# Two edits at a fused transformer kernel's layer hand-overs: order of the low parts, and the last unit by halves

## The reference

```python
# first block
x = x + merged @ w_out                                          # end of hand-over q = 0's input
x = x + square(relu(rmsnorm(x, norm2_g) @ w_up)) @ w_down       # q = 1
# second block, for layer l = 0, 1
x = x + 0.5 * rms_norm(swiglu(rms_norm(x, ng[0]), w_gu, w_down), ng[1])   # q = 2, 5
h = rms_norm(x, ng[2])
mix = concatenate([tok, mem_out]) @ w_o
x = x + rms_norm(mix, ng[3])                                    # q = 3, 6
x = x + 0.5 * rms_norm(swiglu(rms_norm(x, ng[4]), w_gu, w_down), ng[5])   # q = 4, 7
```

## Time and profile before

| | |
|---|---|
| executions | 1473.56, 1477.7, 1473.89 us |
| median | 1473.89 us |
| span of the profiled execution (first to last instruction) | 1470.6 us |
| time of the profiled execution itself | not told by the profile; only its span is |
| mean granted PE clock over the span | 0.982 of full speed |
| PE busy | 1401.7 us, 11538 matmuls |
| DVE, ACT, POOL busy | 922.4, 732.0, 192.7 us |

### The profile page before, as it was taken

One profiled execution on the slowest core, in us unless ns is written; L12 is line 12 of the kernel. 1 busy time (PEld: TensorE's weight loads), 2 busy tenths in 40 slices (PEclk: granted clock), 3 DMA queues, 4 the chain that ended last, 5 costly groups with the idle time before them and its releaser, 6 DMA issues.

```text
span 1470.6 us, 28247 instructions
## 1 busy us (share of the span) xinstructions
PE 1401.7 (95%) x11538; PEld 1358.3 (92%) x11538; DVE 922.4 (63%) x1368; ACT 732.0 (50%) x1205; POOL 192.7 (13%) x210
## 2 busy tenths in 40 slices
PE   5899899999999999999998999999999989899998
PEld 5878799999999999998898999999999987899998
DVE  7998786666535665556765665556564467565644
ACT  7712755544435454455446454455444364554443
POOL 0465000022000111013101111011110010111100
PEclk9899899999999999999999999999999989999999
DMA  9223324455554555544342555544555341345551
GB/s 372 105 103 116 127 86 174 159 204 185 194 185 160 177 195 191 195 173 155 135 144 99 190 197 189 198 172 172 188 198 199 146 170 58 109 178 195 192 200 58
DMA packets 36815, 244.33 MB, mean 166 GB/s; under 512 B 4208, under 2 KB 5360, under 8 KB 8816
## 3 DMA queue, kind: packets, MB, share of 16 engines
q1 hardware_dynamic: 34992, 238.17, 44.7%
q10 hardware_dynamic: 1728, 4.81, 0.9%
HBM read 241.67 MB, written 1.05 MB: 165 GB/s over the span
## 4 chain that ended last, share of the span: by engine, by line
PE 81%; DVE 9%; ACT 5%; issue 2%; POOL 2%; DMA 1%; SPq 0%; DVEq 0%; ACTq 0%; POOLq 0%
PE ps L1891 49%; PE ps L1931 26%; DVE wlo L1083 3%; PE ps L2114 1%; PE ps L2140 1%; ACT whi L592 1%; DVE alo L1478 1%; PE ps L2130 1%; DMA xtok<-in_xt 1%; POOL pr L1809 1%; POOL pr L1808 1%; PE ps L2019 1%; ACT junk L829 1%; DVE yr L1456 0%; ACT pP L782 0%
## 5 line engine op out<-in xcount | busy, mean ns | idle before, releaser
L1083 DVE TENSOR_TENSOR wlo<-raw,whi 128x1024 fp32r<-128x1024 f32 (+1 forms) x434 | 505.1, 1205 | 273.3 <-ACT whi L592 273.2
L1891 PE MATMUL ps<-ahi,whi 128*128 128x256 f32 x2112 | 599.5, 284 | 32.1 <-DVE wlo L1083 18.0
L592 ACT ACTIVATE whi<-raw 128x1024 fp32r<-128x1024 f32 (+1 forms) x434 | 427.2, 1032 | 368.8 <-PE ps L1931 188.1
L1891 PE MATMUL ps<-alo,whi 128*128 128x256 f32 x2112 | 595.4, 282 | 0.0
L1891 PE MATMUL ps<-ahi,wlo 128*128 128x256 f32 x2112 | 594.0, 281 | 0.0
L1891 PEld LDWEIGHTS ps<-ahi,whi 128*128 128x128 f32 x2112 | 403.1, 191 | 38.2 <-issue 23.5
L1891 PEld LDWEIGHTS ps<-alo,whi 128*128 128x128 f32 x2112 | 402.8, 191 | 0.7 <-issue 0.7
L1891 PEld LDWEIGHTS ps<-ahi,wlo 128*128 128x128 f32 x2112 | 401.9, 190 | 0.0
L1829 POOL TENSOR_TENSOR hlo<-fh,hhi 128x256 f32 (+3 forms) x104 | 86.1, 828 | 756.2 <-ACT hhi L899 545.5
L1538 DVE TENSOR_TENSOR fa<-ps,r 128x512 f32<-128x512 f32 x104 | 71.9, 692 | 171.1 <-PE ps L1891 170.9
L1931 PE MATMUL ps<-whi,hhi 128*128 128x256 f32 x960 | 149.1, 277 | 0.0
(11 more groups left out here) (350 smaller groups left out, 1362.9 us busy)
## 6 DMA issues: line engine op xcount, KB each, us to landing
raw<-in_w_gu SPq DMA_DIRECT2D x88, 1024.0 KB, 4.8
raw<-in_w_fd SPq DMA_DIRECT2D x44, 1024.0 KB, 4.8
raw<-in_w_up SPq DMA_DIRECT2D x16, 1024.0 KB, 4.8
raw<-in_w_dn SPq DMA_DIRECT2D x16, 1024.0 KB, 4.8
raw<-in_w_ret SPq DMA_DIRECT2D x13, 1024.0 KB, 4.8
raw<-in_w_mg SPq DMA_DIRECT2D x8, 1024.0 KB, 4.9
raw<-in_w_o SPq DMA_DIRECT2D x8, 1024.0 KB, 6.3
raw<-in_w_mem SPq DMA_DIRECT2D x4, 1024.0 KB, 4.7
```

The lines of the kernel that those rows point to most:

```text
L592: nc.scalar.activation(whi[:, m % SPL, c], raw[:, n % RAW, c], ACT.Copy).then_inc(S("w_hi"), 1)
L1083: ins = tt(wlo[:, m % SPL, c], raw[:, n % RAW, c], whi[:, m % SPL, c].bitcast(F32), ALU.subtract)
L1891: ins = mm(dst, lhsT, rhs, start=k == 0 and p == 0, stop=k == kt - 1 and p == len(pairs) - 1)
```

## The change

It has two parts. In the hand-overs q = 0 to 6 the order of the lows becomes (0,0), (1,0), (0,1), (1,1) in place of (0,0), (0,1), (1,0), (1,1); the order of the highs stays. In the last unit of every `down`, the matmuls of token tile 1 are made in two passes, first those of the chunks 0 and 1 (bank 4), then those of the chunks 2 and 3 (bank 5); a new semaphore `y_left` is raised between the passes. ACT's square of the left half of token tile 1, and DVE's plain_y of it, wait for `y_left` instead of the unit's end.

```diff
@@ ACT, transition(q)
                 def squares_y(t):
-                    act.wait_ge(*y_ready(q, t))
                     for h in range(2):
+                        if t and h == 0:
+                            act.wait_ge(S("y_left"), q + 1)
+                        else:
+                            act.wait_ge(*y_ready(q, t))
                         if q == 7 and h:
                             act.wait_ge(S("y_gain"), 2 * t + 1)
@@ DVE, transition(q)
                 def plain_y(t):
-                    dve.wait_ge(*y_ready(q, t))
                     for h in range(2):
+                        if t and h == 0:
+                            dve.wait_ge(S("y_left"), q + 1)
+                        else:
+                            dve.wait_ge(*y_ready(q, t))
...
                     scale_y(1)
-                    low(0, 0)
                 else:
                     plain_y(0)
                     plain_y(1)
-                    low(0, 0)
-                low(0, 1)
-                low(1, 0)
-                low(1, 1)
+                for h in range(2):
+                    low(0, h)
+                    low(1, h)
@@ PE, down(q, ...)
-                        for kk in range(2):
-                            k = (2 * u + 2 * turn) % (2 * n_units) + kk
-                            pairs = [(whi, high), (whi, low), (wlo, high)]
-                            for p, (wgt, x) in enumerate(pairs):
-                                for c in range(4):
-                                    ws = slice(kk * D + T * c, kk * D + T * c + T)
-                                    ins = mm(two(2 + 2 * t + c // 2)[:, c % 2], x[:, k, xs], wgt[:, n_slot(n), ws],
-                                             start=u + kk + p + c % 2 == 0, stop=u == n_units - 1 and kk == 1 and p == 2,
-                                             skip_group_check=True)
+                        closing = t == 1 and u == n_units - 1
+                        for chunks in ((0, 1), (2, 3)) if closing else (range(4),):
+                            for kk in range(2):
+                                k = (2 * u + 2 * turn) % (2 * n_units) + kk
+                                pairs = [(whi, high), (whi, low), (wlo, high)]
+                                for p, (wgt, x) in enumerate(pairs):
+                                    for c in chunks:
+                                        ws = slice(kk * D + T * c, kk * D + T * c + T)
+                                        ins = mm(two(2 + 2 * t + c // 2)[:, c % 2], x[:, k, xs], wgt[:, n_slot(n), ws],
+                                                 start=u + kk + p + c % 2 == 0, stop=u == n_units - 1 and kk == 1 and p == 2,
+                                                 skip_group_check=True)
+                            if closing and chunks[0] == 0:
+                                ins.then_inc(S("y_left"), 1)
```

## The result

The changed kernel took 1468.33 us (median of 4 runs, 1464.59 to 1469.85) against 1475.66 of the kernel before in the same comparison: ratio 0.9943, 95% interval 0.9921 to 0.9965. A second comparison, 12 runs against 35, gave 0.9969 (0.9951 to 0.9988). Over both, the mean of the 16 runs is 1469.5 and that of the kernel before, whose three comparisons have means from 1474.9 to 1475.6, is 1475.3: about 5.8 us less. I had forecast 2.1 less and a time of 1471.8, between 1468.6 and 1475.0.

The account below looks back on a forecast made before the run. TensorE, busy 95%, was taken as the bound, with seven `alo` waits of 13.2 us; -1.0 (post) + 0.2 + 0.1 (plain) - 1.4 (one drop) = -2.1 us from 1473.89 gave 1471.8, range 1468.6 to 1475.0.

Parts of the forecast that it names:

- second wait at contraction tile 4: Hand-overs, first unit on PE: new wait for `alo` twelve matmuls in, 0.6 to 0.7 us, none where the clock is low.
- The passes cost 0: Closing matmuls in two passes: no price counted for operand loads; upper end 9.0 us.
- q = 7 gives 0: Final hand-over: squaring the left half 1.4 us earlier changes nothing, since the right square waits for VectorE.
- Tile 4: First unit's contraction tile 4: 0.20 us earlier per post hand-over; in q = 0 a 0.67 us stall, 0.23 lost after cover.
- The path's sum, 0.7 us: All hand-overs without the clock: -1.0 us in five post ones, +0.2 and +0.1 in the two plain ones.
- I count one drop fewer, 1.4 us: After first units start: one stretch at 1.2 GHz fewer than four of seven, as PE's first idle stretch gets shorter.
- The upper end: Clock term: three drops to 1.2 GHz fewer behind hand-overs, minus 4.2 us; the opposite end was three more.
- Rival B: Shorter first idle means no drop in clock after any post hand-over: 4.9 us less, 1469.0; chance 0.11.
- Rival A: New order of lows pays in full, ScalarE's highs not limiting: 5.1 us less, 1468.8; chance 0.12.
- D: Rival: extra operand loads of the two closing passes cost time, up to 1482.9 us; chance 0.01.
- C: Rival: ScalarE starts no earlier, tile 4 is released later, three more drops: 5.6 us slower, 1479.5; chance 0.10.
- E: Rival: nothing arrives, bank 4 isn't read earlier and the stall is covered: 1473.9 us; chance 0.06.

Follow-up runs that it names:

- e9: Kernel before, neither part of the change, plus 9 (plain) or 7 (post) identity matmuls on PE ahead of each first unit; 1464.76 us, ratio 0.9935.
- e11: Changed kernel, both parts, plus 10 (plain) or 6 (post) identity matmuls on PE ahead of each first unit; 1465.70 us, ratio 0.9937 to the kernel before.
- e3: Kernel before with only the new order of the lows, no `y_left` and no two passes; 1472.45 us, ratio 0.9992.
- e4: Kernel before with only the two passes and the raise of `y_left`, nobody waiting for it, lows in the old order; 1473.55 us, ratio 1.0003.
- e2: Changed kernel with the lows put back in the old order, two passes and `y_left` waits kept; 1471.09 us, ratio 0.9970 to the kernel before.
- e8: Changed kernel, both parts, with ScalarE's highs also in the new order of the lows; 1471.90 us, ratio 0.9976 to the kernel before.
- e5: Kernel before plus 19 (plain) or 14 (post) identity matmuls ahead of each first unit, overrunning the idle stretch; 1475.09 us, ratio 0.9993.
- e6: Changed kernel with lows in the old order, plus 20 (plain) or 14 (post) identity matmuls ahead of each first unit; 1474.59 us, ratio 1.0000.
- e7: Changed kernel, both parts, plus 20 (plain) or 12 (post) identity matmuls ahead of each first unit; 1470.13 us, ratio 0.9971 to the kernel before.
- e10: Changed kernel with lows in the old order, plus 10 (plain) or 7 (post) identity matmuls ahead of each first unit; 1463.82 us, ratio 0.9942.
- e1: The changed kernel, both parts, run again against the kernel before; 1470.08 us, ratio 0.9969.

## Why the prediction was off

**Right, by its own steps.** In q = 0 the first unit doesn't start earlier (284.52 on the old scale), because low(1, 0) waits for the third high. In post hand-overs it starts 0.85 us earlier (0.88 predicted); the highs start 0.39 earlier (0.38), held by the first transposes of new terms; the idle stretch is 1.49 us (about 1.5). There is a second wait at contraction tile 4 in six of seven hand-overs, and none where the clock is low. VectorE's gap in the lows is 0.67 us (0.7). The passes cost 0, and q = 7 gives 0.

**Sizes that were a little off.** Tile 4 comes 0.32 to 0.37 us earlier than before in post hand-overs with the full clock (0.20 predicted), and 0.54 later in q = 0 (0.67 predicted). One cause: the 1.4 us for twelve matmuls leaves out that the first of them is longer (0.35 against 0.28); before, tile 4 is reached 1.44 to 1.49 us behind the start. The second wait itself is 0.32 or 0.33 us in the trace (0.6 to 0.7 predicted); from the start of the first unit to tile 4 it adds some 0.5. The path's sum, 0.7 us, measured 1.6 at equal clock with a standard error of 0.6, and 0.9 between the second units of e9 and e11, which both have the full clock there.

**The step that failed** is "I count one drop fewer, 1.4 us". The idle stretch of 0.24 and 1.76 us became one of 1.49, and then no post hand-over was followed by the low clock, in two profiles. That is three stretches of 1.41 us fewer, 4.2 us, and the mean clock of all runs says 4.2 us as well. The upper end that I had kept, three fewer, was the value to take. The trace had a hint that I didn't weigh: the same idle time is followed by a drop in three cases and not in two, so the matter is open there and a small change can turn it. I took a third of the cases off, as if the chance fell in proportion to the idle time, for which no row spoke. Rival B, the drops vanish, gave 1469.0 and is what happened, at a chance of 0.11; it should have stood nearer to my forecast's. Rival A is out by VectorE's 0.67 us of waiting for the third high, by the second waits and by e3; D by e4; C by the earlier highs; E by the left square at 658.02 and the first unit 0.85 us earlier.

**Which idle stretch is followed by the low clock.** All thirteen profiles together, us of PE's idle time ahead of the first unit and at tile 4:

| idle of PE | where | followed by a low clock |
|---|---|---|
| 2.17 to 2.47 | plain: before, both edits twice, e2 to e4 | 8 of 12 |
| 0.24 and 1.76 | post: before, e4 | 5 of 10 |
| 1.76 | post: e2 | 2 of 5 |
| 0.24 and 1.27, then 0.33 | post: e3 | 2 of 5 |
| 1.48 or 1.49, then 0.32 to 0.38 | post: both edits twice | 0 of 10 |
| 1.16 to 1.44, then 0.32 to 0.38 | e8, all | 0 of 7 |
| filled | e5 to e7, e9 to e11, all | 0 of 42 |

The shorter stretches are not followed by it and the longer ones are, about every second time. That it takes both edits isn't shown: e3 has the same idle time in sum as both edits (0.24 + 1.27 = 1.51 against 1.49), and its two of five against none of ten is too little to tell from chance; e2's clock in all runs lies between the others. In time e1 and e2 are equal; the cost of the order, 1.3 us on the path, is no larger than what these runs can tell.

**What stays open.** The first profile of the change also has full clock in the latent attention part (1.00 from 1200 to 1260 us, 0.91 in the kernel before), where nothing was changed:

```profile
1200.00:1260.00 60.00, 51.98 (x371) 44.32 (x370) 36.80 (x71) 32.01 (x73) 0.00 (x0) 1.00 0.15 57
```

e1 has 1.00 there too, e2 to e4 0.91 and 0.92, the filled kernels 0.91 to 0.98. Whether what happens in a hand-over spares this part or these profiles were lucky wasn't tried. In return the first profile lost 5.07 us before the first hand-over, also in code that is unchanged; from 30 to 280 us its mean clock is 0.94, and 0.96 in the kernel before. The Trainium skill (TensorE: Matmul & The Clock Gate, Part 1) calls the count of slow matmuls run-variable; the 10 us between the runs of one kernel, with clocks from 0.981 to 0.988, agree. One profile of each kernel is therefore no measure of a gain by clock; the mean clock of all runs is.

## What to carry to other kernels

In this kernel a stretch of 1.5 to 2.5 us in which PE waited cost its own length and then, in 17 of 32 cases, 1.4 us more, as PE ran at 1.2 GHz for a while. Where such a wait can't be shortened, matmuls that nobody needs are worth trying, counted so that they end before the wait does. Before the order of a producer's pieces is changed to suit the consumer, look at what feeds the producer: the new order starts PE earlier, but the second half of what it needs comes later, and here the second unit started 0.29 us later for it (e11 against e10). When an engine's queue is reordered, ask what stands behind each new wait.

## What I had not expected

Filling the idle stretches alone, with no change of the path, makes the kernel 0.9935 (0.9922 to 0.9948) of what it was, though the low stretches that it removes behind the hand-overs are only 5.6 of the 9.6 us. Filling that overran them and delayed each first unit by 1.1 to 1.8 us still cost nothing in all (0.9993). And one float32 matmul of 128 columns is two rows, 0.22 us in a stream of them (in q = 3 of e5 fourteen start at 799.40 and the first unit at 802.45), twice what a transpose of the same size takes (eight in 0.87 us, 658.78 to 659.65).
